# A hybrid trunk step on eight cores: the square of an x block ordered behind earlier copies, the last root moved to ScalarE, and a new order of work

## The chip, the cores and the metric

One Trainium2 chip; the same program runs on 8 cores, each on its own share of the batch. The time is device microseconds (us) of the slowest core, from one launch. TensorE (PE) does the matmuls, VectorE (DVE), ScalarE (ACT) and GpSimd (POOL) the rest; SyncE (SP) issues most transfers.

## The reference

```python
u = rmsnorm(x, norm_mix)                      # 1024 wide
xl, gl, xp, gp, ml, mp = split(u @ w_in)      # 5632 columns
h = rg_lru(causal_conv(xl))                   # gates from block-diagonal w_rg; a = exp(..), sqrt(1 - a*a)
A = h * silu(gl)
B = (pool_means(xp) - xp) @ w_pool * pool_scale * silu(gp)
x = x + (sigmoid(ml) * A + sigmoid(mp) * B) @ w_out
x = x + sigmoid(rmsnorm(x) @ w_ple_gate) * (p @ w_ple)
y = rmsnorm(x, final_norm)
```

16 prompt streams of 2048 frames and 32 sample streams of 32 frames; the states of the convolution, the recurrence and the pooling are outputs too.

## The kernel before

A core has two prompt streams, cut into four tiles of 512 frames each (tiles 0 to 7), and four sample streams of 32 frames as one tile of 128 (tile 8, "the sample"). Every tile goes through three phases. Phase A (`phase_a`) takes x in blocks of 128 frames: load, square with a sum on ScalarE (L865), the reciprocal root as an addition and a power on GpSimd (L834, L836), scaling to bf16 on VectorE (L876), transposition (on TensorE, L882, for tiles 0 and 1; its results are copied from PSUM by ScalarE, L887, or VectorE, L889). Phase B multiplies by w_in, 44 column blocks of 128 with 8 matmuls each (L933; tile 0's first ones in four pieces of 128 frames, so that a piece needs one block of x only). ScalarE reads the results out (silu L989 and L1187, tanh L992, L1023, L1026 and L1190) and does the exponential (L1041) and the root (L1060) of the recurrence, VectorE the convolution (L997), the scan (L1077) and the products. Phase C (`phase_c`), per block of 128 frames: w_out (L1302), the residual add in two halves (L1307), a bf16 copy and a square on ScalarE (L1310, L1314), the gate matmul (L1336) with its tanh (L1340), the product with p @ w_ple (L1343, L1347), the update of x (L1350), a square (L1356), root, scaling by the final norm (L1360) and the output (L1363). The very last block of tile 7 has a function of its own, `last_block`: the gate in four quarters of 256 columns (L1247, tanh L1251, product L1254, update L1257), two squares of 512 (L1262), their sum (L1265), the power on GpSimd (L1268), the multiplication by the norm's weight (L1272), the scaling on ScalarE (L1276) and VectorE (L1280), and two output transfers of half a block (L1285). Blocks are named tile.block: 7.2 is the last block but one.

The order of the instructions is made by a planner, the class `Sched`: each step is a node with an engine, a due time `nom` to which the table ORDER adds a number by tag, and a cost; it places the nodes engine by engine with these costs and the penalties in PRM, and `Z.after` adds an edge to the graph. Each engine then runs its list strictly in order. In the first 45 us of its plan the planner also sets unused matmuls ("fills", L400) before a matmul that would find TensorE idle for over 500 ns. `wg` in PRM ties the first loads of w_in (POOL's queue) to the powers of the x blocks.

ScalarE holds one set of functions at a time (silu and tanh, exponential and tanh, root, logarithm); a change of set is an ACT_TABLE_LOAD. The six buffers `xb` hold the x blocks. E in the prediction is the end of TensorE's last matmul.

## Time and profile before

| what | value |
|---|---|
| median of 3 runs | 975.7 us (975.52 to 977.5) |
| profiled execution | 975.85 us |
| its span, slowest core (core 2) | 974.3 us |
| spans of cores 0 to 7 | 969.4, 973.2, 974.3, 969.2, 972.6, 968.8, 970.0, 973.9 us |
| busy on core 2: TensorE, VectorE, ScalarE, GpSimd | 950.8, 786.6, 773.7, 282.0 us |
| granted TensorE clock, mean, cores 0 to 7 | 0.991, 0.995, 0.989, 0.993, 0.993, 0.993, 0.993, 0.992 |

The profile is of core 2. A timeline row gives start, length, engine, line, operation and tiles; the bracket at its end is the engine's idle time ahead of it and what ended it. Granted clock 1.00 is 2.4 GHz, 0.50 is 1.2 GHz. Idle time of an engine matters only where TensorE, or after its end the last output, waits for it.

### The profile page before, as it was taken

The numbers are of one execution on the slowest core, as the hardware profiler recorded it, in microseconds if no ns is written. First come the engines' busy times: TensorE is split into PE (matmuls) and PEld (weight loads), VectorE is DVE, ScalarE is ACT, GpSimd is POOL, SyncE is SP. The second block draws the span as 40 slices with busy tenths as digits, with TensorE's granted clock in tenths as the row PEclk, the third lists the DMA queues.
The fourth block names the chain that finished last, engine by engine and source line by source line (L and its number), as shares of the span: only waits on it lengthen the run. The fifth ranks groups of instructions, "written<-read, shape, count | busy, mean of one in ns | idle before, by whom it ended". The sixth has DMA issues, their size and how long they took to land.

```text
span 974.3 us, 17207 instructions; the slowest of 8 cores (968.8 to 974.3 us)
## 1 busy us (share of the span) xinstructions
PE 950.8 (98%) x4773; PEld 449.2 (46%) x4773; DVE 786.6 (81%) x1223; ACT 773.7 (79%) x1296; POOL 282.0 (29%) x558
## 2 busy tenths in 40 slices
PE   7999999999999999999999999999999999999996
PEld 5544444444444444444444444444444445455553
DVE  4768979786796969869787897878679698887967
ACT  3799797877978678787696969777697969988764
POOL 3422315113242314312212142322226043211222
PEclk8999999999999999999999999999999999999998
DMA  9999959978955549747785476736756356767633
GB/s 227 166 209 256 217 123 178 187 221 258 263 162 141 186 137 261 211 115 213 218 186 175 143 222 209 215 134 177 222 145 201 98 170 213 218 209 237 192 89 114
DMA packets 111072, 183.13 MB, mean 188 GB/s; under 512 B 65281, under 2 KB 69889, under 8 KB 110978
## 3 DMA queue, kind: packets, MB, share of 16 engines
...
q8 instruction: 41, 0.67, 0.3%
...
## 4 chain that ended last, share of the span: by engine, by line
PE 83%; ACT 6%; issue 5%; DMA 3%; DVE 2%; POOL 0%; SPq 0%; ACTq 0%; DVEq 0%; POOLq 0%
PE psum L933 55%; PE psum L1302 11%; PE psum L1336 10%; PE psum L1343 2%; DMA xb<-xp 2%; DMA wi<-w_rg 1%; PE psum L1020 1%; PE psum L1017 1%; PE psum L1183 1%; ACT wk L1058 1%; ACT wk L1041 1%; ACT wk L1187 0%; ACT L1187 0%; ACT u2t L1314 0%; DVE wk L997 0%
## 5 line engine op out<-in xcount | busy, mean ns | idle before, releaser
L933 PE MATMUL psum<-ut,ring 128*128 128x512 bf16 x2496 | 563.8, 380 | 0.0
L933 PEld LDWEIGHTS psum<-ut,ring 128*128 128x128 bf16 x2496 | 243.6, 98 | 292.4 <-issue 3.5
L997 DVE SCALAR_TENSOR_TENSOR wk<-xw,cvec,wk 128x512 f32<-128x512 f32 x171 | 124.5, 746 | 23.9 <-ACT wk L985 18.8
L1336 PE MATMUL psum<-wpg,u2t 128*128 128x512 bf16 x512 | 119.1, 379 | 1.9 <-ACT wpg L1404 1.5
L1302 PE MATMUL psum<-wout,mg 128*128 128x512 bf16 x512 | 116.7, 379 | 1.1 <-DVE wk L1067 0.7
L834 POOL TENSOR_SCALAR stat<-stat 128x1 f32<-128x1 f32 x98 | 41.8, 428 | 248.4 <-ACT wk L1356 98.8
L933 PE MATMUL psum<-ut,wpg 128*128 128x512 bf16 (+1 forms) x368 | 76.1, 359 | 5.9 <-ACT ut L887 5.8
L1336 PEld LDWEIGHTS psum<-wpg,u2t 128*128 128x128 bf16 x512 | 49.7, 98 | 62.3 <-issue 3.2
L836 POOL TENSOR_TENSOR stat<-stat,negh 128x1 f32<-128x1 f32 x98 | 74.5, 761 | 9.9 <-POOL stat L834 0.4
L1302 PEld LDWEIGHTS psum<-wout,mg 128*128 128x128 bf16 x512 | 49.5, 98 | 60.2 <-issue 2.5
L1082 POOL COPY hst<-wk 128x1 f32<-128x1 f32 x46 | 36.2, 795 | 89.6 <-DVE wk L1077 87.4
L1340 ACT ACTIVATE wk<-psum,stat 128x512 f32<-128x512 f32 x64 | 43.3, 686 | 21.4 <-PE psum L1336 17.7
L983 ACT ACTIVATE xw<-psum 128x512 f32<-128x512 f32 (+1 forms) x72 | 40.8, 567 | 23.9 <-PE psum L933 23.5
L1347 DVE SCALAR_TENSOR_TENSOR wk<-wk,psum 128x512 f32<-128x512 f32 x64 | 43.0, 680 | 18.6 <-PE psum L1343 12.4
L1307 DVE TENSOR_TENSOR xb<-xb,psum 128x512 f32<-128x512 f32 x66 | 44.1, 680 | 17.1 <-PE psum L1302 16.8
L1192 DVE SCALAR_TENSOR_TENSOR wk<-wk 128x512 f32<-128x512 f32 x59 | 40.3, 684 | 20.4 <-ACT wk L1190 14.5
L1077 DVE TENSOR_TENSOR_SCAN wk<-wk,hst 128x512 f32<-128x512 f32 x44 | 55.1, 1271 | 0.2
L1012 DVE SCALAR_TENSOR_TENSOR wk<-wk 128x512 f32<-128x512 f32 x57 | 38.8, 685 | 19.1 <-ACT wk L992 17.0
L933 PEld LDWEIGHTS psum<-ut,wpg 128*128 128x128 bf16 x368 | 34.7, 102 | 41.7 <-issue 7.0
L992 ACT ACTIVATE wk<-psum 128x512 f32<-128x512 f32 x62 | 36.9, 597 | 20.0 <-PE psum L933 18.5
L1029 DVE SCALAR_TENSOR_TENSOR wk<-wk 128x512 f32<-128x512 f32 x55 | 37.7, 686 | 18.4 <-ACT wk L1026 18.4
L989 ACT ACTIVATE wk<-psum 128x512 f32<-128x512 f32 x57 | 33.9, 602 | 21.5 <-PE psum L933 20.1
...
## 6 DMA issues: line engine op xcount, KB each, us to landing
...
```

Source lines behind the costliest of these rows:

```text
L834: nd("pool", 120, lambda e: e.tensor_scalar(out=st.ap[:, 1:2], in0=st.ap[:, 0:1], scalar1=float(D) * EPS, scalar2=None, op0=ALU.add), read ...
L836: return nd("pool", 510, lambda e: e.tensor_tensor(out=st.ap[:, 1:2], in0=st.ap[:, 1:2], in1=NEGH.ap, op=ALU.pow), reads=[st, NEGH], write ...
L933: nd("pe", pe_cost(8, N // cuts), [lambda e, kc=kc, a=a, z=z: e.matmul(b.ap[:, a:z], lhsT=s.ap.rearrange("p (k n) -> p k n", k=8)[:, kc, o ...
L983: nd("act", act_cost(N), lambda e: e.activation(out=xw()[:, :, 3:W], in_=xl(), func=AF.Copy), reads=[b_xl], writes=[X], nom=nom)
L997: nd("dve", dve_cost(N), lambda e, j=j, w=w: e.scalar_tensor_tensor(out=av(), in0=xw()[:, :, 3 - j:W - j], scalar=w, in1=av(), op0=ALU.mul ...
L1077: nd("dve", 64 + 2.17 * L, lambda e, a2=a2, aa=aa, ti=ti, sg=sg, init=init: e.tensor_tensor_scan(out=a2.ap[:, sg * L:(sg + 1) * L], data0= ...
L1192: nd("dve", dve_cost(N), lambda e: e.scalar_tensor_tensor(out=tm.ap[:, 0:N], in0=tm.ap[:, 0:N], scalar=1.0, in1=tg.ap[:, 0:N], op0=ALU.add ...
L1302: nd("pe", pe_cost(8, 512), [lambda e, hf=hf, kc=kc, d=d, j=j: e.matmul(d[hf].ap, lhsT=mg_v()[:, kc, j * 128:(j + 1) * 128], rhs=wout_v[:, ...
L1307: nd("dve", dve_cost(512), lambda e, hf=hf, xr=xr, d=d: e.tensor_tensor(out=xr.ap[:, hf * 512:(hf + 1) * 512], in0=xr.ap[:, hf * 512:(hf + ...
L1336: nd("pe", pe_cost(8, 512), [lambda e, hf=hf, kc=kc, eb=eb, u2t=u2t: e.matmul(eb[hf].ap, lhsT=u2t.ap.rearrange("p (k n) -> p k n", k=8)[:, ...
L1340: nd("act", act_cost(512, ptrs=1), lambda e, hf=hf, eb=eb, tg=tg, st=st: e.activation(out=tg[hf].ap, in_=eb[hf].ap, func=AF.Tanh, scale=st ...
L1347: nd("dve", dve_cost(512), lambda e, hf=hf, tg=tg, fk=fk: e.scalar_tensor_tensor(out=tg[hf].ap, in0=tg[hf].ap, scalar=1.0, in1=fk[hf].ap, ...
```

## The change

1. For tiles 0 and 1, the square of x block n gets an edge behind the PSUM copies of block n-2.
2. `last_block`: five column pieces (256, 256, 256, 128, 128) instead of four, three squares (512, 256, 256) instead of two; a dummy root on ScalarE behind the last tanh, so that the function set changes there; the reciprocal root is a root on ScalarE (its bias takes the sum of the first two squares, L1278 in the new file) and a reciprocal on VectorE, instead of GpSimd's power; the second half is scaled and multiplied by the norm's weight in one instruction.
3. The final scaling of the sample and of blocks 7.1 and 7.2 is cut in two halves; those of 7.2 get an edge behind the last update of x in `last_block`.
4. `xb` buffers are tracked in three parts instead of two. PRM and ORDER have new numbers throughout; the threshold for fills goes from 300 to 700. The loads of x go out for blocks 0, 3, 1, 2, 4, 5 (buffers xb0 to xb5, ahead of the small vectors `vecs`) instead of 0 to 4, `vecs`, 5. The gate weights (wa, wi) are issued ahead of the sixth load of w_in instead of behind it. Between the first chunks of tile 0 there are 2 or 3 fills where there were 6 or 7.

```diff
-PRM = dict(window=76081.776, lim=113076.056, lag=10050.77, penw=1.548, slack=4.921, evac=0, p2=0, c2=0.552, a2=0.944,
+PRM = dict(window=76473.092, lim=113076.056, lag=10050.77, penw=0.2, slack=36.991, evac=0, p2=0, c2=0.552, a2=0.944,
...
-           wg=[-1, 0, 2, 4, 5, 6, 7], wbn=40452.849, fl=45000.0, fm=300.0, nr=5, nu=3, nx=3, ac=3)
+           wg=[-1, 0, 2, 4, 5, 6, 7], wbn=40452.849, fl=45000.0, fm=700.0, nr=5, nu=3, nx=3, ac=3)
...
-ORDER = {"a0.0": -5265, "a0.1": -847, "a0.2": -2424, "a0.3": -3738, "a1.0": -288, "a1.1": -96, "a1.2": 1144,
+ORDER = {"a0.0": -59225, "a0.1": -3618, "a0.2": -5347, "a0.3": -43337, "a1.0": -5941, "a1.1": 25, "a1.2": 3642,
...
-    mkpool("xb", 6, [128, 1024], F32, nsub=2)
+    mkpool("xb", 6, [128, 1024], F32, nsub=3)
...
+            if S["idx"] < 2:
+                Z.after(n_, *evac_first.get(len(pow_first) - 2, ()))
...
+                    if S["idx"] < 2:
+                        evac_first.setdefault(len(pow_first) - 1, []).append(n_)
...
+        edge = (0, 256, 512, 768, 896, 1024)
+        part = (0, 0, 1, 2, 2)
+        for q in range(5):
+            a, z, t_, sub = edge[q], edge[q + 1], tq[q], (xr, part[q])
+            hf, o, w = a // 512, a % 512, z - a
...
-            nd("dve", dve_cost(w), lambda e, q=q, t_=t_: e.scalar_tensor_tensor(
-                out=xr.ap[:, q * w:(q + 1) * w], in0=t_.ap[:, 0:w], scalar=0.5,
-                in1=xr.ap[:, q * w:(q + 1) * w], op0=ALU.mult, op1=ALU.add),
-               reads=[t_, (xr, hf)], writes=[(xr, hf)], nom=nom)
-            if q % 2 == 1:
-                nd("act", act_cost(512, False, acc=True), lambda e, hf=hf: e.activation(
-                    out=junk.ap, in_=xr.ap[:, hf * 512:(hf + 1) * 512], func=AF.Square,
-                    accum_out=acc[hf].ap[:, 0:1]), reads=[(xr, hf)], writes=[junk, acc[hf]], nom=nom)
+            nd("dve", dve_cost(w), lambda e, t_=t_, a=a, z=z: e.scalar_tensor_tensor(
+                out=xr.ap[:, a:z], in0=t_.ap[:, 0:z - a], scalar=0.5, in1=xr.ap[:, a:z], op0=ALU.mult, op1=ALU.add),
+               reads=[t_, sub], writes=[sub], nom=nom)
+        n_d = Z.nodes[-1]
+        for n_ in ends:
+            Z.after(n_, n_d)
+        n_ = nd("act", 210, lambda e: e.activation(out=T16.ap[:, 0:1], in_=CV2.ap[:, BPS:BPS + 1], func=AF.Sqrt, scale=0.0),
+                reads=[CV2], writes=[T16], nom=nom, tset=T_SQRT)
+        Z.after(n_, n_t)
+        n_t = n_
+        for k, (a, z) in enumerate(((0, 512), (512, 768), (768, 1024))):
+            n_ = nd("act", act_cost(z - a, False, acc=True), lambda e, k=k, a=a, z=z: e.activation(
+                out=junk.ap[:, 0:z - a], in_=xr.ap[:, a:z], func=AF.Square, accum_out=acc[k].ap[:, 0:1]),
+                    reads=[(xr, k)], writes=[junk, acc[k]], nom=nom)
+            Z.after(n_, n_t)
...
-            op0=ALU.add, op1=ALU.add), reads=list(acc), writes=[acc[0]], nom=nom)
-        nd("pool", 510, lambda e: e.tensor_tensor(out=acc[0].ap[:, 1:2], in0=acc[0].ap[:, 1:2], in1=NEGH.ap, op=ALU.pow),
-           reads=[acc[0], NEGH], writes=[acc[0]], nom=nom)
+            op0=ALU.add, op1=ALU.add), reads=list(acc[0:2]), writes=[acc[0]], nom=nom)
+        nd("act", 230, lambda e: e.activation(out=acc[2].ap[:, 0:1], in_=acc[2].ap[:, 0:1], func=AF.Sqrt,
+                                              bias=acc[0].ap[:, 1:2]), reads=[acc[0], acc[2]], writes=[acc[2]], nom=nom,
+           tset=T_SQRT)
+        nd("dve", 110, lambda e: e.reciprocal(out=acc[2].ap[:, 1:2], in_=acc[2].ap[:, 0:1]), reads=[acc[2]],
+           writes=[acc[2]], nom=nom)
+        h_, h2 = slice(0, 512), slice(512, 1024)
...
-        nd("dve", dve_cost(512, True, ptr=1), lambda e, h2=h2: e.tensor_scalar(
-            out=xr.ap[:, h2], in0=xr.ap[:, h2], scalar1=acc[0].ap[:, 1:2], scalar2=None, op0=ALU.mult),
-           reads=[(xr, 1), acc[0]], writes=[(xr, 1)], nom=nom)
+        nd("dve", dve_cost(512, ptr=1), lambda e: e.scalar_tensor_tensor(
+            out=xr.ap[:, h2], in0=xr.ap[:, h2], scalar=acc[2].ap[:, 1:2], in1=G3.ap[:, h2], op0=ALU.mult, op1=ALU.mult),
+           reads=[(xr, 1), (xr, 2), acc[2], G3], writes=[(xr, 1), (xr, 2)], nom=nom)
...
+            cuts = 2 if S["idx"] == 8 or (S["idx"] == 7 and j >= 1) else 1
+            for k in range(cuts):
+                h_ = slice(k * 1024 // cuts, (k + 1) * 1024 // cuts)
+                xk = xb2(xr)[k:k + 1] if cuts == 2 else xb2(xr)
+                n_ = nd("dve", dve_cost(1024 // cuts), lambda e, xr=xr, st2=st2, h_=h_: e.scalar_tensor_tensor(
+                    out=xr.ap[:, h_], in0=xr.ap[:, h_], scalar=st2.ap[:, 1:2], in1=G3.ap[:, h_], op0=ALU.mult, op1=ALU.mult),
+                   reads=xk + [st2, G3], writes=xk, nom=nom)
+                if S["idx"] == 7 and j == 2:
+                    ends.append(n_)
```

The new file's lines are 2 higher from L787 on, 4 from the copies on (L887 is L891), 6 from phase B on (L933 is L939, L1077 is L1083, L1187 is L1193) and 14 in phase C (L1336 is L1350); L1302 is L1317, L1307 is L1322, L1310 is L1325, L1360 is L1378.

ScalarE in the opening, before; wout is a place for the squares' unused output, ut0 the transposed input of tile 0, and block n is in buffer xb n:

```order
L865 ACTIVATE wout,stat0<-xb0 128x1024
L865 ACTIVATE wout,stat1<-xb1 128x1024
L865 ACTIVATE wout,stat2<-xb2 128x1024
L887 ACTIVATE ut0<-psum 128x4x128
L865 ACTIVATE wout,stat3<-xb3 128x1024
L887 ACTIVATE ut0<-psum 128x4x128
L865 ACTIVATE wout,stat4<-xb4 128x1024
L887 ACTIVATE ut0<-psum 128x4x128
L865 ACTIVATE wout,stat5<-xb5 128x1024
L887 ACTIVATE ut0<-psum 128x4x128 x2
```

and in the new order, where block 3 is in xb1, block 1 in xb2 and block 2 in xb3:

```order
L867 ACTIVATE wout,stat0<-xb0 128x1024
L891 ACTIVATE ut0<-psum 128x4x128 x2
L867 ACTIVATE wout,stat1<-xb2 128x1024
L867 ACTIVATE wout,stat2<-xb3 128x1024
L891 ACTIVATE ut0<-psum 128x4x128 x2
L867 ACTIVATE wout,stat3<-xb1 128x1024
L891 ACTIVATE ut0<-psum 128x4x128
L867 ACTIVATE wout,stat4<-xb4 128x1024
L891 ACTIVATE ut0<-psum 128x4x128 x2
L867 ACTIVATE wout,stat5<-xb5 128x1024
```

Both copies of block 0 stand ahead of the second square, both copies of block 1 on ScalarE behind the squares of blocks 1 and 2, and block 3's square behind them.

VectorE about the second residual add of the block that ScalarE copies at the start of the sample's projections (ws, mgs are the sample's tiles), before:

```order
L1088 SCALAR_TENSOR_TENSOR ws<-ws 128x128 x2
L1350 SCALAR_TENSOR_TENSOR xb<-wk,xb 128x512
L1307 TENSOR_TENSOR xb<-xb,psum 128x512
L1192 SCALAR_TENSOR_TENSOR ws<-ws 128x128 x2
L1195 SCALAR_TENSOR_TENSOR mgs<-psum,cvec,ws 128x128 x2
L1091 TENSOR_TENSOR mgs<-mgs,ws 128x128 x2
L1307 TENSOR_TENSOR xb<-xb,psum 128x512
L1012 SCALAR_TENSOR_TENSOR wk<-wk 128x512
```

and in the new order:

```order
L1364 SCALAR_TENSOR_TENSOR xb<-wk,xb 128x512
L1083 SCALAR_TENSOR_TENSOR ws<-ws,sc 128x32 x2
L1322 TENSOR_TENSOR xb<-xb,psum 128x512
L1083 SCALAR_TENSOR_TENSOR ws<-ws,sc 128x32 x2
L1198 SCALAR_TENSOR_TENSOR ws<-ws 128x128
L1094 SCALAR_TENSOR_TENSOR ws<-ws 128x128
L1083 SCALAR_TENSOR_TENSOR ws<-ws,sc 128x32
L1201 SCALAR_TENSOR_TENSOR mgs<-psum,cvec,ws 128x128
L1322 TENSOR_TENSOR xb<-xb,psum 128x512
L1097 TENSOR_TENSOR mgs<-mgs,ws 128x128
L1094 SCALAR_TENSOR_TENSOR ws<-ws 128x128
L1378 SCALAR_TENSOR_TENSOR xb<-xb,stat,g3bc 128x1024
```

Two each of L1192, L1195 and L1091 stood between the two adds; one L1198 and one L1201 (the same steps) and parts of the sample's scans stand there now, and the rest of the sample comes behind the second add.

VectorE from the last block's products to its end, before:

```order
L1254 SCALAR_TENSOR_TENSOR wk<-wk,psum 128x256 x2
L1257 SCALAR_TENSOR_TENSOR xb<-wk,xb 128x256
L1254 SCALAR_TENSOR_TENSOR wk<-wk,psum 128x256
L1257 SCALAR_TENSOR_TENSOR xb<-wk,xb 128x256 x2
L1254 SCALAR_TENSOR_TENSOR wk<-wk,psum 128x256
L1257 SCALAR_TENSOR_TENSOR xb<-wk,xb 128x256
L1360 SCALAR_TENSOR_TENSOR xb<-xb,stat,g3bc 128x1024
L1265 TENSOR_SCALAR stat<-stat 128x1
L1272 TENSOR_TENSOR xb<-xb,g3bc 128x512 x2
L1280 TENSOR_SCALAR xb<-xb,stat 128x512
```

and in the new order:

```order
L1260 SCALAR_TENSOR_TENSOR wk<-wk,psum 128x256
L1263 SCALAR_TENSOR_TENSOR xb<-wk,xb 128x256
L1260 SCALAR_TENSOR_TENSOR wk<-wk,psum 128x256
L1263 SCALAR_TENSOR_TENSOR xb<-wk,xb 128x256
L1260 SCALAR_TENSOR_TENSOR wk<-wk,psum 128x256
L1260 SCALAR_TENSOR_TENSOR wk<-wk,psum 128x128 x2
L1263 SCALAR_TENSOR_TENSOR xb<-wk,xb 128x256
L1378 SCALAR_TENSOR_TENSOR xb<-xb,stat,g3bc 128x512 x2
L1263 SCALAR_TENSOR_TENSOR xb<-wk,xb 128x128 x2
L1378 SCALAR_TENSOR_TENSOR xb<-xb,stat,g3bc 128x512 x2
L1278 TENSOR_SCALAR stat<-stat 128x1
L1287 TENSOR_TENSOR xb<-xb,g3bc 128x512
L1284 RECIPROCAL stat<-stat 128x1
L1292 SCALAR_TENSOR_TENSOR xb<-xb,stat,g3bc 128x512
```

The sum (L1265, now L1278) has two scalings in halves ahead of it, the sample's and block 7.2's, where it had the sample's alone; the reciprocal and the product of the second half stand at the end.

## Rows read from the trace of the kernel before

**Rows 1.** The page: busy time by engine, and the chain that ended last.

```profile
PE 950.8 (98%) x4773; PEld 449.2 (46%) x4773; DVE 786.6 (81%) x1223; ACT 773.7 (79%) x1296; POOL 282.0 (29%) x558
...
PE 83%; ACT 6%; issue 5%; DMA 3%; DVE 2%; POOL 0%; SPq 0%; ACTq 0%; DVEq 0%; POOLq 0%
```

**Rows 2.** Spans and mean granted clock by core.

```profile
core 2: 974.3 us, clock 0.989
...
core 7: 973.9 us, clock 0.992
```

**Rows 3.** Timeline of core 7, ScalarE and TensorE in the opening; columns as told above.

```profile
17.99 1.06 ACT L865 ACTIVATE wout<-xb 128x1024 bf16<-128x1024 f32 x1 [2.93 <-DMA xb<-xp]
...
19.04 0.58 ACT L887 ACTIVATE ut<-psum 128x512 bf16<-128x512 bf16 x1
...
19.88 1.87 PE L933 MATMUL psum<-ut,wpg 128*128 128x128 bf16 x16 [2.37 <-ACT ut L887]
...
22.39 0.95 PE L400 MATMUL psum<-uts 128*128 128x128 bf16 x7
...
23.27 1.07 PE L933 MATMUL psum<-ut,wpg 128*128 128x128 bf16 x16
...
25.89 0.61 PE L933 MATMUL psum<-ut,wpg 128*128 128x128 bf16 x8 [0.58 <-ACT ut L887]
```

**Rows 4.** Timeline of core 2, TensorE at the first gates.

```profile
46.91 0.59 PE L1020 MATMUL psum<-xcb,wi 128*128 128x512 bf16 x2 [1.10 <-DMA wi<-w_rg]
```

**Rows 5.** Timeline of core 2, TensorE at the sample's projections.

```profile
876.02 1.89 PE L933 MATMUL psum<-ut,ring 128*128 128x512 bf16 x8
...
881.32 0.61 PE L933 MATMUL psum<-uts,ring 128*128 128x128 bf16 x8 [2.21 <-ACT wk L1187]
...
882.67 3.16 PE L933 MATMUL psum<-ut,ring 128*128 128x512 bf16 x8
```

**Rows 6.** Busy times by engine in the window there, with granted clock, DMA share, GB/s.

```profile
880.00:885.00 5.00, 3.68 (x23) 2.28 (x24) 3.91 (x8) 2.57 (x7) 0.00 (x0) 0.68 0.35 110
```

**Rows 7.** Timeline of core 2, ScalarE ahead of that wait and behind it.

```profile
862.37 1.06 ACT L1310 ACTIVATE ub<-xb 128x1024 bf16<-128x1024 f32 x1 [0.33 <-DVE xb L1307]
...
880.58 0.60 ACT L1187 ACTIVATE wk<-psum 128x512 f32<-128x512 f32 x1
881.08 0.44 ACT L989 ACTIVATE ws<-psum 128x128 f32<-128x128 f32 x2
```

**Rows 8.** Timeline of core 2, VectorE ahead of it.

```profile
860.25 0.48 DVE L1192 SCALAR_TENSOR_TENSOR ws<-ws 128x128 f32<-128x128 f32 x2
...
861.60 0.67 DVE L1307 TENSOR_TENSOR xb<-xb,psum 128x512 f32<-128x512 f32 x1
```

**Rows 9.** Timeline of core 2, ScalarE about a table load.

```profile
867.69 0.63 ACT L1190 ACTIVATE wk<-psum 128x512 f32<-128x512 f32 x1
868.34 1.28 ACT L1041 ACT_TABLE_LOAD   x1
869.64 0.82 ACT L1041 ACTIVATE wk<-wk,cvec 128x512 f32<-128x512 f32 x1
```

**Rows 10.** Window behind that wait; columns as in rows 6.

```profile
886.00:946.00 60.00, 60.00 (x392) 31.68 (x390) 48.79 (x105) 48.14 (x97) 13.43 (x27) 1.00 0.61 190
```

**Rows 11.** Timeline of core 2 from the last block's gate on.

```profile
961.05 3.66 PE L1247 MATMUL psum<-wpg,u2t 128*128 128x256 bf16 x32
...
965.37 0.46 ACT L1251 ACTIVATE wk<-psum,stat 128x256 f32<-128x256 f32 x1
...
966.99 1.28 DVE L1360 SCALAR_TENSOR_TENSOR xb<-xb,stat,g3bc 128x1024 f32<-128x1024 f32 x1
967.23 0.63 ACT L1262 ACTIVATE wk<-xb 128x512 f32<-128x512 f32 x1 [0.53 <-DVE xb L1257]
...
968.19 0.21 DVE L1265 TENSOR_SCALAR stat<-stat 128x1 f32<-128x1 f32 x1
...
969.50 0.72 ACT L1276 ACTIVATE xb<-xb,stat 128x512 f32<-128x512 f32 x1 [1.55 <-POOL stat L1268]
...
970.34 0.33 SPq L1285 DMA_DIRECT2D yp<-xb  x1
```

More of the change, by code:

```diff
@@ L780, in build_program @@
     pow_first = []
+    evac_first = {}
     w_first = []
+    ends = []
     w_wait = []
@@ L1238, in last_block @@
                reads=[pt] + WPE, writes=[fk[hf]], nom=nom)
-        tq = [tg[0], tg[1], Z.val("wk"), Z.val("wk")]
-        banks = [eb[0], eb[1], Z.val("fb"), Z.val("fb")]
-        acc = Z.val("stat"), Z.val("stat")
+        tq = [tg[0], tg[1], Z.val("wk"), Z.val("wk"), Z.val("wk")]
+        banks = [eb[0], eb[1], Z.val("fb"), Z.val("fb"), Z.val("fb")]
+        acc = Z.val("stat"), Z.val("stat"), Z.val("stat")
         junk = Z.val("wk")
         Z.tag = "cf%d.%d" % (S["idx"], j)
-        for q in range(Q):
-            hf, o = q // 2, (q % 2) * w
-            t_ = tq[q]
-            nd("pe", pe_cost(8, w), [lambda e, q=q, kc=kc: e.matmul(
-                banks[q].ap[:, 0:w], lhsT=u2t.ap.rearrange("p (k n) -> p k n", k=8)[:, kc, :],
-                rhs=wpg_v[:, kc, q * w:(q + 1) * w], start=(kc == 0), stop=(kc == 7)) for kc in range(8)],
+        edge = (0, 256, 512, 768, 896, 1024)
@@ L1250, in last_block @@
+        part = (0, 0, 1, 2, 2)
+        for q in range(5):
+            a, z, t_, sub = edge[q], edge[q + 1], tq[q], (xr, part[q])
+            hf, o, w = a // 512, a % 512, z - a
+            nd("pe", pe_cost(8, w), [lambda e, q=q, kc=kc, a=a, z=z: e.matmul(
+                banks[q].ap[:, 0:z - a], lhsT=u2t.ap.rearrange("p (k n) -> p k n", k=8)[:, kc, :],
+                rhs=wpg_v[:, kc, a:z], start=(kc == 0), stop=(kc == 7)) for kc in range(8)],
                reads=[u2t] + WPG, writes=[banks[q]], nom=nom)
-            nd("act", act_cost(w, ptrs=1), lambda e, q=q, t_=t_: e.activation(
+            n_t = nd("act", act_cost(w, ptrs=1), lambda e, q=q, t_=t_, w=w: e.activation(
@@ L1296, in phase_c @@
             Z.tag = "cl%d.%d" % (S["idx"], j)
-            load(xr, x_src(S, j), nom - 10000, 1650)
+            end_ = S["idx"] == 7 and j == 3
+            sub = lambda hf: [(xr, 0)] if hf == 0 else [(xr, 1), (xr, 2)] if end_ else [(xr, 1)]
+            xrs = sub(0) + sub(1)
+            load(xr, x_src(S, j), nom - 10000, 1650, into=xrs)
             load(pt, p_src(S, j), nom - 10000, 600, queue="pool")
@@ L1314, in phase_c @@
             nd("act", act_cost(1024, False, acc=True), lambda e, xr=xr, st=st, u2t=u2t: e.activation(
[L1315 removed]
+                out=u2t.ap, in_=xr.ap, func=AF.Square, accum_out=st.ap[:, 0:1]), reads=xrs, writes=[st, u2t], nom=nom)
             rstd_ops(st, nom)
[L1317 removed]
             if S["idx"] >= 7 and j >= nt - 1:
```

44 lines of the change are left out of this document (16 added, 28 removed), and 126 rows, old and new, of the table ORDER.

## The prediction

> **What bounds the kernel now.** I read the engine totals of the page first: TensorE is busy 950.8 of 974.3 us and the chain that ended last is TensorE's for 83% [rows 1], so no more than some 23 us can move at all: the opening, the few places where TensorE waits, and the tail after its last matmul. The spans by core come next [rows 2]: core 2 ends last (974.3), core 7 only 0.4 earlier. A gain on one core is thus worth 0.4 unless core 7 gets it too, and each term below is worked out for both. The profiled execution took 975.85 us, 1.55 more than its span; the median of the runs is 975.7, so the sum is made against 975.85 and carries over. Then I read the timeline at the three places that the diff touches: the opening, the stretch in which the sample tile's projections start, and the tail; the rows stand with each part below.
>
> **Opening.** On core 7 the fourth x block lands and is squared at 17.99; only then, at 19.04, can ScalarE copy the second half of block 1, and TensorE, which needs it, starts that block's projections at 19.88 [rows 3]: 0.26 after the copy's end (19.04 + 0.58). (A chunk below is the projections of one 128-token block of the first tile.) The edit moves the square of block n behind the copies of block n-2. Block 3's square goes behind the copies of block 1, but block 3 is now loaded second, and block 2's x comes fourth; its square is still ahead of block 1's copies, and there are now two of them on ScalarE where one was done by VectorE. So chunk 1 starts one copy later: 19.88 + 0.5 = 20.4. What gives it back: the fills between its successor's transposes and the next projections are three instead of seven, and seven took 0.95, so four are worth 0.5. Chunk 2 is then where it was. Chunk 3 (25.89, after a wait for its copies) depends on block 3's chain on VectorE, which has become later by up to the same 0.5. Bounds: 0 if the fills pay for all, +0.5 if none. I take the middle, +0.3. The other piece is core 2's alone: its TensorE stood 1.10 for the second gate weight [rows 4], which is now issued ahead of a block of w_in instead of behind it; the trace of core 7 has no such wait, so there it is worth nothing. On core 2: -1.1 (0 if the landing is set by the queues' load and not by the issue).
>
> **The sample's projections.** After 879.1 TensorE stands 2.21 us until ScalarE's silu copy L1187 frees a bank; the clock granted in 880 to 885 is then 0.68 on average (between the two levels, 1.00 for 2.4 GHz and 0.50 for 1.2), and eight 512-column matmuls take 3.16 where eight before the gap took 1.89 [rows 5, 6]. So the place costs 2.21 + 1.27 = 3.48. The trace of every core has the same 2.21 there. ScalarE is the cause: from 862.37 to 881.18 it never rests [rows 7]. In the new order the same kinds of work stand between that place and the first silu, with as many function-table fetches. Two things differ. First, the start: it waited for the second residual add of VectorE, which stood behind two each of L1192, L1195 and L1091 of the sample; from the first of them (860.25) to the add (861.60) is 1.35 [rows 8]. Now about half of the sample's work is still to come when the add runs, and I count 1.3 less ahead of it. Second, the first silu after the fetch is 128 columns wide instead of 512: two of the narrow ones took 0.44 and one wide one 0.60 [rows 7], so about 0.35 sooner. 2.21 - 1.3 - 0.35 leaves some 0.6 of idle; since smaller waits can appear around it I take 1.0, and 0.15 for what is left of the clock's fall, 1.15 in place of 3.48: -2.3. Bounds: 0, if ScalarE's stretch starts no sooner, and -3.5.
>
> **More table fetches.** Counting the changes of function set along ScalarE's new order, there are two more between this place and the tail. A fetch takes 1.28 [rows 9], so 2.57 of ScalarE time. From 886 to 946 ScalarE is busy 48.14 of 60 us and TensorE waits for nothing [rows 10]: 11.9 us of cover. I cost them at nothing; without cover they are 2.57 and, if the clock falls again, 1.27 more.
>
> **Tail.** TensorE ends at E = 964.71 (961.05 + 3.66), the last tanh at E+1.12, the last output is issued at E+5.63 and the span ends 4.0 after that [rows 11]. After E everything is on the path. What goes: GpSimd's power and the trip to it, and half of the multiplications by the norm's weight ahead of the end. What comes: a table fetch (1.28), a dummy root and the last root on ScalarE, a reciprocal, and on VectorE the final scaling of block 7.2, which stood before the quarter loop and is now tied behind the last update of x.
> ScalarE: the last tanh, 128 columns, ends at about E+1.0; the fetch to E+2.3, the dummy root (some 0.2, like the one-column sum of [rows 11]) to E+2.5; the squares (0.63 for 512 columns [rows 11], an estimate of 0.2 more for reading out the sum, and of 0.5 in all for 256) end at 3.3, 3.7 and 4.2.
> VectorE: fifth gate product to E+1.55, third update to 1.95, the sample's scaling in two halves (1.28 as one piece, [rows 11]) to 3.2, the last two updates to 3.65, the two halves of block 7.2 to 4.85, and only then the sum (0.2) to 5.05. Before, the sum was at E+3.48 to 3.69 and its only company was the sample's scaling. From 5.05: root to 5.35, meanwhile one multiplication (0.67) to 5.7, reciprocal to 5.85, the two last scalings (0.72, [rows 11]) to 6.65, issue at E+6.7. That is 1.07 behind before: +1.0. So the new root is not what costs: the squares are ready at 4.2 and wait for VectorE, and the 1.28 of block 7.2 decides. Bounds: +0.3, if the halves of both scalings overlap at their ends and the root finds the sum at once; +1.7, if block 7.2's output, now issued 1.8 ahead of the last ones, also delays their landing.
> A row speaks on the fetch's true price: the tanh copy L1190 ends at 868.32, the fetch starts at 868.34 and the next activation at 869.64 [rows 9], so it costs 1.30 in all. The Trainium skill (ScalarE: Activation LUTs, What ACT_TABLE_LOAD costs) gives 1283 ns for the load and about 1380 ns more to drain, some 2.66 us for every change of set. By that the squares would end at 4.6, 5.1 and 5.5, the root would wait for the third one, and the tail would be +1.2 instead of +1.0, an estimate. The load agrees with this trace (1.28); the drain does not show in it.
>
> **The sum.** Core 7: 973.9 + 0.3 - 2.3 + 1.0 = 972.9. Core 2: 974.3 + 0.3 - 1.1 - 2.3 + 1.0 = 972.2. Core 7 ends last, 1.4 under the old span: 975.85 - 1.4 = 974.4 us.
>
> **Rivals.**
> A: the stall of the sample goes whole and the tail pays little. For it: the wait is one single wait, 2.21 long, and 1.65 of it I found. Against: ScalarE's stretch holds as much work as before. Core 7: 973.9 - 3.5 + 0.3 = 970.7, core 2 the same or less: 972.3 us.
> B, on the other side: the two added fetches are not covered. Place: the sample's last batches, where a narrow silu, an exponential and a root now alternate within a few instructions, with TensorE behind them for banks. Price: 2 x 1.28 = 2.57 of idle, and 1.27 for the clock: 974.4 + 3.8 = 978.2; with half of it 976.3. It decides where ScalarE has less than 1.5 us in hand at the batches, for then the slower clock comes on top. For it: the same chain (fetch, silu, bank) made the 2.21. Against: the 11.9 us of idle.
> C: the opening's edit does not do what its name says, and worse. Block 2's square still holds block 1's copies, and with fewer fills TensorE's clock comes up later: core 7's chunk 1 took 1.87 and its chunk 2, by then at nearly the full clock, 1.07 [rows 3], so 3 us of work done at half speed costs 1.5. That gives 974.4 + 1.5 = 975.9.
>
> **Chances.** The forecast 0.38, A 0.30, B 0.20, C 0.12. A measurement of this kernel can tell about 0.2%, 1.95 us, from no change. The forecast's own range is 972.8 to 976.0: most of it is within 0.2% (0.30), a part faster (0.08). A is faster, B slower, C within but for 0.02. Together: faster 0.38, within 0.2% 0.40, slower 0.22. The range reaches to A with its tail bound and to nearly all of B: 971.6 to 978.0.
>
> **What would show it.** Right, if in the new profile the sum of the last block stands behind both halves of block 7.2's scaling and starts near E+4.9, with the squares done before it; if TensorE's wait before the sample's matmuls is about 1 us, with a clock near 1.00 in the 5 us after; if the projections of block 1 start near 20 us and not near 16; and if core 2 no longer waits for the gate weight. Wrong, if a wait of 2 us or more stands on TensorE anywhere after 60 us, if the last issue is under E+6 or over E+7.4, or if the span of core 7 moves by more than 2.5 us.

## The result, and the profile after

The changed kernel takes 983.97 us (median of 6, lowest 981.88) where the kernel before takes 976.55 in the same comparison: ratio 1.0063, 95% interval 1.004 to 1.0087. It is slower by some 0.6%, outside the range, where 974.4 was forecast. Two of the six executions, above 1114 us, had one die at a lower clock; the ratios here leave such executions out. The profiled execution took 982.34 us. On the page, where [rows 1] stood, TensorE does the same work in a longer span, and the chain has more DMA in it (5% for 3%):

```profile
PE 950.6 (97%) x4755; PEld 446.3 (46%) x4755; DVE 785.6 (80%) x1226; ACT 782.0 (80%) x1307; POOL 283.4 (29%) x557
...
PE 81%; ACT 6%; DMA 5%; issue 4%; DVE 3%; SPq 0%; DVEq 0%; ACTq 0%; POOL 0%; POOLq 0%
```

The spans by core, for [rows 2], say more. Core 7 is 1.0 shorter than before and the other seven are longer. Of each neighbour pair one core ends some 5 us after its mate (3.8 to 5.1 in the profile before). Which one it is changes from one execution to the next (in another one core 7 took 984.0 and core 6 978.6): core 7 was the later of its pair in the profile before and is the earlier one here. Compared by this role, the earlier cores are +5.0 on average and the later ones +5.9:

```profile
core 0: 978.4 us, clock 0.996
core 1: 973.4 us, clock 0.994
core 2: 980.4 us, clock 0.993
core 3: 975.6 us, clock 0.992
core 4: 980.8 us, clock 0.995
core 5: 975.6 us, clock 0.996
core 6: 978.0 us, clock 0.997
core 7: 972.9 us, clock 0.994
```

To find the place, the span is cut into stages and TensorE's busy time compared (first busy column). The first fence is core 4 of before, the second core 4 of after, the third core 7 of after:

```profile
300.00:460.00 160.00, 159.08 (x738) 72.02 (x737) 131.65 (x183) 129.18 (x208) 44.33 (x88) 1.00 0.61 181
460.00:860.00 400.00, 399.56 (x1963) 185.03 (x1962) 331.22 (x519) 324.18 (x545) 118.72 (x221) 1.00 0.62 185
```

```profile
300.00:460.00 160.00, 154.31 (x706) 69.13 (x705) 126.70 (x176) 125.32 (x202) 41.73 (x88) 0.99 0.67 183
460.00:860.00 400.00, 399.05 (x1935) 183.49 (x1933) 327.00 (x498) 320.59 (x537) 118.35 (x216) 1.00 0.60 180
```

```profile
300.00:460.00 160.00, 159.24 (x738) 71.90 (x737) 133.49 (x186) 129.23 (x210) 44.54 (x92) 1.00 0.65 190
```

On core 4, the later core of its pair in both profiles, the stage from 300 to 460 has 4.8 us more idle; the next 400 us only 0.5. Core 7 has 0.8 of idle there. In that stage of core 4, TensorE stands three times for about 2 us (for a transpose that lands late, for a chain that the trace puts down to ScalarE, for a load of pt), and after the third its clock falls: eight 512-column matmuls take 3.54 at 441.35 where as many take 1.89 a little later. The fall is on this core alone; cores 0, 2 and 6 wait 1.57 to 1.87 for pt and keep their clock. None of these waits was in the kernel before. The timeline of TensorE, core 4:

```profile
322.08 3.61 PE L1350 MATMUL psum<-wpg,u2t 128*128 128x512 bf16 x16 [1.81 <-DMA u2t<-ub]
...
366.62 3.61 PE L939 MATMUL psum<-ut,ring 128*128 128x512 bf16 x16 [1.86 <-ACT wk L1064]
...
440.46 1.10 PE L1357 MATMUL psum<-wpe,pt 128*128 128x512 bf16 x4 [2.03 <-DMA pt<-pp]
441.35 3.54 PE L939 MATMUL psum<-ut,ring 128*128 128x512 bf16 x8
...
444.95 1.89 PE L939 MATMUL psum<-ut,ring 128*128 128x512 bf16 x8
```

The timeline of GpSimd, which issues the load of pt, and the window behind the third wait (columns as in [rows 6]):

```profile
432.89 0.62 POOL L699 DMA_DIRECT2D pt<-pp  x1 [0.21 <-POOL stat L836]
```

```profile
440.00:445.00 5.00, 4.54 (x14) 1.74 (x15) 2.34 (x3) 2.30 (x4) 0.00 (x0) 0.66 1.00 345
```

Issued at 432.89, pt is wanted at 440.46 - 2.03 = 438.43: a lead of 5.5 us, on every core. The landing took 7.0, 6.9, 7.3 and 6.9 us on cores 0, 2, 4 and 6, 6.1 on core 5 and 5.0 on cores 1, 3 and 7. So core 5 waits 0.82, cores 0, 2, 4 and 6 wait 1.6 to 2.0, and the three others not at all. Before, the shortest lead of a pt load between 60 and 940 us was 9.4; behind 940 two were under 6 and cost no wait, since the loads land in 2.4 to 2.7 there.

At the sample, for [rows 5] and [rows 6], the long wait is gone and the clock stays at 1.00, but several small waits stand in its place (core 4):

```profile
866.20 1.89 PE L939 MATMUL psum<-ut,ring 128*128 128x512 bf16 x8 [0.23 <-DVE xb L1322]
...
883.11 1.89 PE L939 MATMUL psum<-ut,ring 128*128 128x512 bf16 x8 [0.70 <-DVE wk L1361]
...
886.58 0.61 PE L939 MATMUL psum<-uts,ring 128*128 128x128 bf16 x8 [0.69 <-ACT ws L995]
...
892.35 0.22 PE L1023 MATMUL psum<-xcb,wa 128*128 128x128 bf16 x1 [0.41 <-DVE mg L1201]
```

```profile
883.00:888.00 5.00, 4.21 (x37) 2.66 (x38) 3.60 (x10) 4.97 (x12) 2.17 (x4) 1.00 0.45 109
```

The opening of core 7, for [rows 3]: chunks 1 and 3 start 0.76 and 0.75 sooner than before.

```profile
19.12 1.86 PE L939 MATMUL psum<-ut,wpg 128*128 128x128 bf16 x16 [1.94 <-ACT ut L891]
...
25.14 2.78 PE L939 MATMUL psum<-ut,wpg 128*128 128x128 bf16 x24 [0.73 <-ACT ut L891]
```

The tail of core 4, for [rows 11]. TensorE ends at E = 965.91 + 3.68 = 969.59:

```profile
965.91 3.68 PE L1253 MATMUL psum<-wpg,u2t 128*128 128x256 bf16 x40
...
970.33 1.28 ACT L1269 ACT_TABLE_LOAD   x1
...
971.63 0.20 ACT L1269 ACTIVATE t<-cvec 128x1 f32<-128x1 f32 x1
...
972.45 0.33 SPq L1383 DMA_DIRECT2D ys<-xb  x1
...
972.90 1.41 DVE L1378 SCALAR_TENSOR_TENSOR xb<-xb,stat,g3bc 128x512 f32<-128x512 f32 x2
...
973.46 0.19 ACT L1274 ACTIVATION_READ_ACCUMULATOR wk<-xb 128x1 f32 x1
974.22 0.21 DVE L1278 TENSOR_SCALAR stat<-stat 128x1 f32<-128x1 f32 x1
...
976.03 0.38 ACTq L1297 DMA_DIRECT2D yp<-xb  x1
976.83 0.33 SPq L1383 DMA_DIRECT2D yp<-xb  x1
977.26 0.41 SPq L1297 DMA_DIRECT2D yp<-xb  x1
```

The two halves of block 7.2's scaling end at 974.31, but its output (L1383) is issued on SyncE only at 976.83, 4.05 us after the sample's output ys was issued (972.45 + 0.33), and the last output stands behind it at E+7.67. `finalize` puts one wait for each of 72 DMA lanes ahead of SyncE's second-to-last operation (`i == len(ops) - 2`). Before, that operation was ys, and the row of waits lay in time in which SyncE had nothing to issue. Now it is block 7.2's output.

### The profile page after: what moved, and what is told of

It reads as the page before. It is cut to its first block, busy times and chain, and to the rows that moved or that the text cites. A ratio compares the mean times of both kernels' runs of the same rounds, so it can differ in the third digit from the quotient of the medians.

```text
span 980.8 us, 17143 instructions; the slowest of 8 cores (972.9 to 980.8 us)
## 1 busy us (share of the span) xinstructions
PE 950.6 (97%) x4755; PEld 446.3 (46%) x4755; DVE 785.6 (80%) x1226; ACT 782.0 (80%) x1307; POOL 283.4 (29%) x557
## 4 chain that ended last, share of the span: by engine, by line
PE 81%; ACT 6%; DMA 5%; issue 4%; DVE 3%; SPq 0%; DVEq 0%; ACTq 0%; POOL 0%; POOLq 0%
PE psum L939 55%; PE psum L1317 10%; PE psum L1350 9%; DMA xb<-xp 3%; PE psum L1357 2%; PE psum L1023 1%; PE psum L1189 1%; PE psum L1026 1%; DMA u2t<-ub 1%; DMA pt<-pp 1%; ACT wk L1047 1%; ACT wk L1064 1%; DVE wk L1003 1%; ACT u2t L1329 0%; ACT wk L1354 0%
## 5 line engine op out<-in xcount | busy, mean ns | idle before, releaser
L939 PE MATMUL psum<-ut,ring 128*128 128x512 bf16 x2432 | 548.2, 380 | 3.2 <-ACT wk L1064 1.9
L939 PEld LDWEIGHTS psum<-ut,ring 128*128 128x128 bf16 x2432 | 237.3, 98 | 289.2 <-issue 7.6
L1003 DVE SCALAR_TENSOR_TENSOR wk<-xw,cvec,wk 128x512 f32<-128x512 f32 x177 | 128.4, 746 | 25.7 <-ACT wk L991 18.0
L1350 PE MATMUL psum<-wpg,u2t 128*128 128x512 bf16 x512 | 118.7, 379 | 2.2 <-DMA u2t<-ub 2.2
L1317 PE MATMUL psum<-wout,mg 128*128 128x512 bf16 x512 | 116.5, 379 | 0.9 <-issue 0.7
L939 PE MATMUL psum<-ut,wpg 128*128 128x512 bf16 (+1 forms) x432 | 90.6, 365 | 6.1 <-ACT ut L891 3.2
L1088 POOL COPY hst<-wk 128x1 f32<-128x1 f32 x46 | 50.7, 1105 | 125.0 <-DVE wk L1083 121.2
L1350 PEld LDWEIGHTS psum<-wpg,u2t 128*128 128x128 bf16 x512 | 49.6, 98 | 62.1 <-issue 3.8
L1317 PEld LDWEIGHTS psum<-wout,mg 128*128 128x128 bf16 x512 | 49.5, 98 | 60.7 <-issue 2.7
L838 POOL TENSOR_TENSOR stat<-stat,negh 128x1 f32<-128x1 f32 x98 | 71.6, 732 | 8.9 <-POOL stat L836 1.1
L939 PEld LDWEIGHTS psum<-ut,wpg 128*128 128x128 bf16 x432 | 41.6, 103 | 49.4 <-issue 7.0
L1198 DVE SCALAR_TENSOR_TENSOR wk<-wk 128x512 f32<-128x512 f32 x57 | 38.9, 685 | 27.5 <-ACT wk L1196 22.5
L1083 DVE TENSOR_TENSOR_SCAN wk<-wk,hst 128x512 f32<-128x512 f32 x45 | 56.3, 1271 | 0.3
L880 DVE SCALAR_TENSOR_TENSOR ub<-xb,stat,gmbc 128x1024 bf16<-128x1024 f32 (+1 forms) x37 | 42.7, 1162 | 12.9 <-POOL stat L838 12.8
L1018 DVE SCALAR_TENSOR_TENSOR wk<-wk 128x512 f32<-128x512 f32 x57 | 38.6, 684 | 16.0 <-ACT wk L998 8.2
L1322 DVE TENSOR_TENSOR xb<-xb,psum 128x512 f32<-128x512 f32 x66 | 44.0, 679 | 9.0 <-PE psum L1317 8.5
```

The lines of the kernel that those rows point to most:

```text
L838: return nd("pool", 510, lambda e: e.tensor_tensor(out=st.ap[:, 1:2], in0=st.ap[:, 1:2], in1=NEGH.ap, op=ALU.pow), reads=[st, NEGH], write ...
L880: nd("dve", dve_cost(w, ptr=1), lambda e, x=x, u=u, st=st, h_=h_: e.scalar_tensor_tensor(out=u.ap[:, h_], in0=x.ap[:, h_], scalar=st.ap[:, ...
L939: nd("pe", pe_cost(8, N // cuts), [lambda e, kc=kc, a=a, z=z: e.matmul(b.ap[:, a:z], lhsT=s.ap.rearrange("p (k n) -> p k n", k=8)[:, kc, o ...
L1003: nd("dve", dve_cost(N), lambda e, j=j, w=w: e.scalar_tensor_tensor(out=av(), in0=xw()[:, :, 3 - j:W - j], scalar=w, in1=av(), op0=ALU.mul ...
L1083: nd("dve", 64 + 2.17 * L, lambda e, a2=a2, aa=aa, ti=ti, sg=sg, init=init: e.tensor_tensor_scan(out=a2.ap[:, sg * L:(sg + 1) * L], data0= ...
L1088: nd("pool", 100, lambda e, a2=a2, c=c: e.tensor_copy(out=HST[c].ap, in_=a2.ap[:, N - 1:N]), reads=[a2], writes=[HST[c]], nom=nom + k)
```

## The experiments

Beside the ratios I use the mean span of the eight cores over a kernel's executions, set against that of the kernel before on the same chip: a program whose slowest core changes from one execution to the next shows small differences there more surely. The first four kernels ran on one chip, whose runs of before scattered (975.1 to 988.6 us, mean span 973.17) and lay higher than those above (median 979.96 for 976.55), so that ratios there come out some 0.3% lower; the others ran on a second (971.47 and 971.57). Twice the standard error of a difference of mean spans is 0.3 to 0.65 us, and 1.25 for the kernel with three executions. The changed kernel itself ran on neither chip, so what a cure gains on it can only be set against the other kernels here.

**The new plan alone**: before's code with the new numbers, about:

```diff
-PRM = dict(window=76081.776, ...
+PRM = dict(window=76473.092, ...
-ORDER = {"a0.0": -5265, ...
+ORDER = {"a0.0": -59225, ...
```

> The code of before (no edge for the squares, old last block, GpSimd's power) with the new PRM and ORDER. Theory P (the new plan costs, through waits of TensorE in the middle of the run: for the transposed u2t near 322 us, for L1064 near 366, for pt near 440 with a fall of the clock): the three waits stand, TensorE ends 4 to 5 us later than before's 964.7, the tail keeps before's 9.6, so 980 to 981 us, ratio 1.004 to 1.005. Theory T (the new tail costs most, the waits in the middle are mostly chance): 975 to 977 us, ratio within 0.001 of 1. Theory G (the edge for the squares costs in the opening): as T.

Measured: 982.11 us, ratio 1.0011 (0.9982 to 1.004), where theory P had 1.004 to 1.005; by itself this says little. The mean span is 976.52, +3.35. The waits of core 5 (us in total, times, longest):

```profile
PE psum L1336 <- DMA u2t<-ub: 2.6, 2, 2.1
...
PE psum L1343 <- DMA pt<-pp: 2.1, 1, 2.1
PE psum L933 <- DMA ring<-win_bf: 1.7, 1, 1.7
```

They are the waits of after, at 324, 442 and 368 us, with none of the edited code in the kernel. The numbers alone bring them. But they are not all that the plan costs: by role the earlier cores of the pairs are +3.2 and the later ones +3.5, and in the first 60 us of its profile TensorE is idle for 10.2 on the mean of the cores, where it was 7.9 before.

**The new tail alone**, on the old plan and without the opening's edge:

```diff
+        edge = (0, 256, 512, 768, 896, 1024)
+        part = (0, 0, 1, 2, 2)
+        for n_ in ends:
+            Z.after(n_, n_d)
```

> The new code of the last block and of the final scalings with the old PRM and ORDER and without the edge for the squares. Theory P: only the tail is longer, by the 1.6 us that lie between 9.6 and 11.2 from TensorE's end to the span's end in the profiles: 977 to 977.5 us, ratio 1.001 to 1.002, and no wait for pt near 440. Theory T: 980 to 982 us, ratio 1.005 or more.

Measured: 980.65 us, ratio 0.9993 (0.9957 to 1.0029), mean span +1.26. No pt wait near 440; the 2.21 of the sample stands on every core. The span ends E+11.5 to 11.9 instead of E+9.6.

**After without the square's edge:**

```diff
-            if S["idx"] < 2:
-                Z.after(n_, *evac_first.get(len(pow_first) - 2, ()))
```

> The changed kernel without the edge that puts the square of block n behind the copies of block n-2; all else, with PRM and ORDER, stays. Theory P: the waits in the middle stay and the time is that of the changed kernel within 1 us: 981.5 to 983.5, ratio to before 1.005 to 1.007. Theory G: the opening gets shorter by 2 us or more, ratio 1.004 or less.

Measured: 984.92 us, ratio 1.0025 (0.9995 to 1.0055), mean span +5.09; pt waits of 1.4 to 2.4 on cores 1, 3, 5 and 7, the tail E+11.4. Theory P had 981.5 to 983.5 us and 1.005 to 1.007; the time is above it, and the ratio below it by about what this chip's before takes off. So the edge is not what makes after slow; plan (+3.35) and tail (+1.26) give 4.6 of the 5.1.

**After, with the row of waits one operation earlier on SyncE:**

```diff
-                if final and i == len(ops) - 2:
+                if final and i == len(ops) - 3:
```

> The changed kernel with SyncE's row of some 70 waits on finished transfers one place earlier in its queue: ahead of the sample's output instead of ahead of block 7.2's. Theory W (going through these waits takes SyncE some 4 us, which now lie between the sample's output at 972.45 and block 7.2's at 976.83 and hold back the last half block): the last issue falls from 7.7 us behind TensorE's end to about 6.4, and the time by 1.0 to 1.3 us against the changed kernel, ratio 1.005 instead of 1.006. Rival theory L (the last output's landing is set by the transfers ahead of it, not by the issue): the issue comes earlier, the span by less than 0.4 us.

Measured: 983.34 us, ratio 1.0000 (0.9967 to 1.0033), mean span +3.73, 1.4 less than without the edge. The ratio of theory W, 1.005, was missed; its issue at E+6.4 (6.47) came out, and so did its gain of 1.0 to 1.3, nearly, if the run without the edge stands for after. SyncE's and ScalarE's last issues, core 5:

```profile
975.26 0.34 SPq L1383 DMA_DIRECT2D ys<-xb  x1
...
977.19 0.33 SPq L1383 DMA_DIRECT2D yp<-xb  x1
...
978.84 0.41 ACTq L1297 DMA_DIRECT2D yp<-xb  x1
978.87 0.33 SPq L1297 DMA_DIRECT2D yp<-xb  x1
```

Block 7.2's output now goes out 0.08 after its scaling ends (977.11), both last outputs go out together, and the span ends E+9.5 to 9.6 on every core instead of E+11.2 to 11.6. The excess of the tail was that row of waits.

**After, with GpSimd issuing that pt load as soon as its buffer is free:**

```diff
+    o = next(n for n in Z.nodes if n.tag == "cl3.0" and n.queue == "pool").ops[0]
+    i = max(P.ops.index(d) for d in o.deps)
+    k = next(k for k in range(i, len(P.ops)) if P.ops[k].eng == "pool")
+    P.ops.remove(o)
+    P.ops.insert(k, o)
```

> The changed kernel with one transfer moved: GpSimd issues the pt of block 3.0 four of its instructions sooner, as soon as its buffer is free, some 10 us ahead of where the new plan has it (it is needed 5.5 us after its issue, and on the later core of a pair of neighbours it took 7.3 to land). Theory P: TensorE's wait for pt near 440 us (1.4 to 2.4 on one core of each pair) and the fall of the clock behind it go; the slowest cores gain 2 to 3.5 us, the time falls to 979.5 to 981, ratio to before on this chip 0.998 to 1.001 where the changed kernel would have 1.003. Rival theory R (the later core of a pair is late for good: what it does not wait for here it waits for at the next transfer): the wait goes and the span stays within 1 us.

Measured: 980.2 us, ratio 1.0033 (1.0019 to 1.0047), mean span 975.85, +4.38; the time is as theory P had it, its ratio (to 1.001) was missed. GpSimd and TensorE, core 2:

```profile
429.51 0.62 POOL L699 DMA_DIRECT2D pt<-pp  x1 [2.96 <-PE psum L1357]
...
440.24 0.81 PE L1357 MATMUL psum<-wpe,pt 128*128 128x512 bf16 x3
440.89 1.89 PE L939 MATMUL psum<-ut,ring 128*128 128x512 bf16 x8
```

Issued 10.5 to 10.7 us ahead instead of 5.5, pt is there, and there is no wait and no fall of the clock behind it on any core. The load also lands sooner: in 2.5 to 3.3 us, where it took 5.0 to 7.3 when issued 5 us later. So the early issue gave both a longer lead and a shorter landing; why the landing is shorter there was not tried. Waits for u2t at 322 (1.6 to 2.6, on five cores) and for the ring at 368 stay.

**Before with only the edge, planned anew with the old numbers:**

```diff
+            if S["idx"] < 2:
+                Z.after(n_, *evac_first.get(len(pow_first) - 2, ()))
...
+                    if S["idx"] < 2:
+                        evac_first.setdefault(len(pow_first) - 1, []).append(n_)
```

> The kernel before with nothing but the edge that puts the square of block n behind the copies of block n-2; its loads go out for blocks 0, 1, 2, 3 in order. Theory O (the edge does what its name says only where the loads are in order): ScalarE copies block 1 ahead of the square of block 3, so chunk 1 starts near 16 to 17 us where it was 18 to 20.5; chunk 3 stays bound by the fourth block's landing, so the continuous work starts 0 to 1 us sooner and the time moves by 0 to -1 us, ratio 0.999 to 1. Rival theory G (the edge costs in any plan): the time rises by 1 us or more, ratio 1.001 or more.

Measured: 984.84 us, ratio 1.0084 (1.0069 to 1.01), mean span +7.1. Chunk 1 starts at 14.2 to 16.4, some 3.5 us or more sooner than in [rows 3], chunk 3 at 23.3 to 25, and far more is lost elsewhere. TensorE, core 2:

```profile
428.22 2.29 PE L938 MATMUL psum<-ut,ring 128*128 128x512 bf16 x5 [2.65 <-ACT wk L1192]
```

This wait stands at 423 to 431 us on every core, 400 us behind the edit: the planner's later choices came out differently. The 2.21 at the sample stays.

**Before with the tail at its best**: the new tail on the old plan, no edge, block 7.2's scaling not tied, the row of waits one earlier:

```diff
-                if final and i == len(ops) - 2:
+                if final and i == len(ops) - 3:
...
-        for n_ in ends:
-            Z.after(n_, n_d)
```

> The old PRM and ORDER, no edge for the squares, the new last block, but block 7.2's scaling not tied behind the last update, and SyncE's row of some 70 waits one place earlier. Theory W: the sum no longer waits for 7.2's scaling and the last output no longer for the row of waits: last issue at E+5.2 to 5.6 where the new code had E+7.9 in the old plan, and the tail from TensorE's end to the span's end 8.7 to 9.6 where it was 11.6; time within 0 to -1 us of before, ratio 0.999 to 1. Rival theory L (the landing of the outputs sets the end): the tail stays above 10.5.

Measured: 978.38 us, ratio 1.0005 (0.9991 to 1.0018), mean span 971.45, -0.02; the span ends E+9.5 for E+9.6. The root on ScalarE gains nothing even with everything cured. **With the edge added to it** (diff as for the edge above):

> Gate_only and tail_best together: all code of the change but the tie of 7.2's scaling, with the old PRM and ORDER, and the row of waits one place earlier. Theories O and W: no wait of 1 us or more for u2t, pt or the ring in the middle that the kernel before has not, tail 8.7 to 9.6, time 0 to -2 us against before, ratio 0.998 to 1. Were the new code itself what makes the waits in the middle, they would be here too, and the ratio 1.003 or more.

Measured: ratio 1.0083 (1.0059 to 1.0107), from three executions of 982.5 to 986.7 us, mean span +6.6; the same 2.65 at 424 on core 2. Theories O and W are wrong here: it is again the plan that the edge sets off.

**The edge without a new plan**: in before's finished order only ScalarE's copies of blocks 0 and 1 go ahead of the squares of blocks 2 and 3.

```diff
+    put_behind(4, 5, 1)
+    put_behind(6, 7, 1)
```

> The kernel before with the edge's effect alone and nothing planned anew: ScalarE's copy of block 0 stands ahead of the square of block 2 and its copy of block 1 ahead of the square of block 3; every other instruction keeps its place. Theory O: chunk 1 starts near 15 to 17 us (it was 18 to 20.5), the continuous work 0.5 to 1.5 us sooner, no new wait in the middle, time -0.5 to -1.5 us, ratio 0.9985 to 0.9995. Rival theory G (the edge costs in itself, as gate_only's 1.008 would say): 1.003 or more.

Measured: 979.3 us, ratio 1.0004 (0.9984 to 1.0025), mean span +0.8. TensorE, core 7:

```profile
14.30 1.05 PE L933 MATMUL psum<-ut,wpg 128*128 128x128 bf16 x16 [0.42 <-ACT ut L887]
...
21.37 1.86 PE L933 MATMUL psum<-ut,wpg 128*128 128x128 bf16 x16 [4.28 <-ACT ut L887]
...
24.99 1.01 PE L933 MATMUL psum<-ut,wpg 128*128 128x128 bf16 x8 [0.26 <-ACT ut L887]
```

Chunk 1 starts 5.6 sooner than in [rows 3], and TensorE then stands 4.28 for chunk 2; chunk 3 is where it was, within 0.9. The later blocks set the opening, so the edge by itself is worth nothing, and neither theory's time came.

**The sample's wait alone**: in before's order two roots on ScalarE (L1060, at 876) go behind, to just ahead of the exponential at 891.

```diff
+    put_behind(1006, 1030, 2)
```

> The kernel before with two of ScalarE's roots (L1060, of tile 7) moved from 876 us to just ahead of the exponential at 891, and nothing else; so the fetch of the root's table and the return to silu's no longer stand ahead of the sample's first silu. Theory S (ScalarE's chain sets the wait of 2.21 us and the clock's fall of 1.27 behind it, on every core): the wait falls under 0.5 us, the granted clock in the 5 us behind it is near 1, every core is 2.5 to 3.5 us shorter, ratio 0.9965 to 0.9975. Rival theory D (the wait comes back a few us later, since the roots are now late for VectorE): less than 1 us, ratio 0.999 or more.

Measured: 978.15 us, ratio 0.9996 (0.9979 to 1.0012), mean span +0.5. TensorE, core 0:

```profile
874.60 0.61 PE L933 MATMUL psum<-uts,ring 128*128 128x128 bf16 x8 [1.42 <-ACT wk L1187]
...
893.46 0.22 PE L1017 MATMUL psum<-xcb,wa 128*128 128x128 bf16 x1 [1.57 <-ACT xcb L1008]
```

```profile
893.00:898.00 5.00, 3.98 (x14) 1.57 (x15) 2.82 (x7) 4.92 (x10) 1.15 (x2) 0.74 0.44 53
```

The wait shrinks from 2.21 to 1.42, and what is saved comes back 19 us later, as theory D had it. On this core and on core 4 the clock falls there (0.74 and 0.69 in that window); on the other six, behind the same wait of 1.57, it stays at 1.00. **Both of these edits together:**

> Gate_swap and sqrt_later together, on the kernel before. If both theories (O and S) hold, the gains add: 3 to 5 us, ratio 0.995 to 0.997, the fastest of all kernels here. If the later core of each pair of neighbours is held by transfers anyway (rival R), the sum is under 2 us, ratio 0.998 or more.

Measured: 977.8 us, ratio 1.0009 (0.9986 to 1.0032), mean span +1.1. There were no gains to add.

**After with both cures** (the early pt load and the early row of waits; diffs as above):

> The changed kernel with pt of block 3.0 issued sooner and the row of waits one place earlier (pt_hoist and waits_early together). Theories P and W: both gains add, 2 to 3.5 us and 1.8 us, so 977.5 to 979 where before has 976 to 978: ratio 1.001 to 1.002; what is left against before is the wait for u2t near 322 us. Rival R: the gains do not add, ratio 1.003 or more.

Measured: 979.26 us, ratio 1.0015 (1.0 to 1.0029), mean span +3.05. Against +4.38 with the pt load alone cured, the tail's cure takes 1.3. What is left are waits for u2t at 320 to 324 (up to 2.4), for the ring near 368 (up to 2.5) and some 2 us of small ones at the sample. No version beat the kernel before.

## Why the prediction was wrong

**The middle: the step that failed.** The prediction has terms for the opening, the sample and the tail, and none for the middle: it let the trace of before hold there for a plan whose every number is new. The new plan gives a transpose of u2t and a pt load leads that these transfers do not keep to, on the later core of a pair above all (with the plan alone u2t is 1.2 to 2.2 late on cores 1, 4 and 7 too). For core 4, the core that ends last, the end of TensorE moved by 969.59 - 963.04 = +6.6 against its own trace of before. Of it the stage from 300 to 460 gives 159.08 - 154.31 = 4.8 of idle and 3.54 - 1.89 = 1.65 of slower clock, together 6.4; what the other stages lose and gain there comes to nearly nothing. Over all eight cores the idle from 60 to 860 us, which the prediction put at no change, grew by 3.1 on average. That the plan and not the code brings the waits is shown by the plan alone; that pt's issue is the cause of its wait is shown by its early load. For the waits near 322 and 367 it is only read from the trace, and for the second not even clear which work came last: on core 4 of after the trace names ScalarE (L1064), with the plan alone it names the weights of the ring. No run issued these sooner.

The plan itself counts a pt load at 2.0 us and 0.9 ahead of it, against 5.0 to 7.3 measured, at a DMA share of 0.76 to 0.93 while it ran. The Trainium skill (DMA: Bandwidth & Descriptors, Anatomy of one DMA — SWDGE (gpsimd) path) has about the same price, 2.0 us and the bytes at 436 GB/s: an estimate of 2.2 for these 64 KB. The measurement decides here: that price held on no core at that place, and the early load's 2.5 to 3.3 come near it.

**The sample.** -2.3 was forecast. The mechanism was right: the wait went, and with it the fall of the clock (1.00 in the window). The allowance of 1.0 for smaller waits was too small. On core 4 they are 0.23 + 0.70 + 0.69 + 0.41 and two of 0.25 later, 2.5 in all in place of 3.48: -1.0. Nor was 3.48 the price on every core: the 2.21 stands on all eight, but on cores 3 and 5 of before the clock did not fall behind it. Core 3 of before:

```profile
877.76 0.61 PE L933 MATMUL psum<-uts,ring 128*128 128x128 bf16 x8 [2.21 <-ACT wk L1187]
...
878.71 1.89 PE L933 MATMUL psum<-ut,ring 128*128 128x512 bf16 x8
```

With the new tail alone the same 2.21 left the clock up on seven cores of eight. ScalarE's stretch kept its work, as rival A's counter-argument had it, and the run with two roots moved shows the same thing: what is taken from one wait there returns in the next.

**The tail.** +1.0 was forecast, and the steps on the engines came out: squares done before the sum (973.65), the sum at E+4.63 (forecast 4.85), ScalarE's last output issued at E+6.44 (6.7). SyncE's last issue was forecast for the same moment and came at E+7.67, outside the E+7.4 named as a bound. The span ended E+9.6 on seven cores before (10.1 on core 7) and ends E+11.2 to 11.6 now: +1.6 to +2.0, and +1.1 on core 7. The step that failed here is that I followed the engines and not SyncE's queue, where the order of the last outputs decides whose issue carries the 72 waits. The run with these waits one operation earlier took the excess away. On the table fetch, the next activation follows the start of the load by 1.30 and the third square ends at E+4.06, where 4.2 was forecast without a drain: here the further 1380 ns of the Trainium skill (ScalarE: Activation LUTs, What ACT_TABLE_LOAD costs), by which it would be 5.5, do not show either.

**The opening.** +0.3 was forecast with bounds of 0 and +0.5. Taking the changes of TensorE's idle in the later stages, and the clock falls, from the move of its end leaves -0.8 on core 7, +0.6 on core 4 and +1.5 on core 2, and +1.2 on the mean of the eight cores: wider than my bounds, and mis-sized. With the plan alone TensorE is idle there even longer (10.2 for 7.9), so the new numbers and not the edge are the likely cause; no run separates their parts. Chunk 1 came at 19.12 and not at 20.4, but near 20 rather than 16: the name of the edit is not its effect, as rival C said, and the swap without a new plan shows that even a chunk 1 at 14.3 gains nothing. C's other half, a clock that comes up later, did not show: the granted clock of the first 60 us is 0.98 on the mean of the cores, for 0.95 before. The wait for the gate weight on core 2 [rows 4] is gone, as forecast.

**The table fetches** cost little, where nothing was forecast: between 892 and the tail there is no TensorE wait over 0.7, and TensorE's idle from 900 to its end is 0.8 on the mean of the cores, for 0.1 before. How much of that is theirs is not shown.

**The rivals.** A had the sample's wait going whole, and small ones took its place; its tail of +0.3 came to +1.6 to +2.0. B had the right sign and the right price (a fresh idle of over 2 us and a clock fall) but the wrong place and cause: not ScalarE's fetches near the sample but DMAs 440 us earlier; its condition, less than 1.5 us in hand on ScalarE, came from no row. The prediction's own test, a wait of 2 us or more on TensorE after 60 us, is what fired (2.03 at 440 on core 4; 2.24 at 321 on core 0). On core 7, which meets none of these waits, TensorE ends 2.1 sooner (961.63 for 963.76), and -2.0 was forecast. That agreement is luck: core 7 was the later of its pair before and is the earlier now. Against the earlier core of the same pair before (core 6, 960.41) it is +1.2, and over the four pairs TensorE's end moved by +3.3 on the earlier cores and +4.2 on the later ones. So the sum held for no core, and with 8 cores it has to be made for each role in a pair, not for a core by its number.
